# A decoder layer with product-key experts: the second half of the tokens computes every expert in dense matmul steps instead of gathering its own

## What is computed

```python
def peer_ffn(h, w_q, keys1, keys2, u_tab, v_tab):
    q = (hf @ w_q).astype(jnp.float32).reshape(tokens, PEER_HEADS, 2, PEER_HALF)
    s1 = jnp.einsum('thd,hnd->thn', q[:, :, 0], keys1.astype(jnp.float32))
    s2 = jnp.einsum('thd,hnd->thn', q[:, :, 1], keys2.astype(jnp.float32))
    v1, i1 = lax.top_k(s1, PEER_TOPK)
    v2, i2 = lax.top_k(s2, PEER_TOPK)
    ...
    top_score, pos = lax.top_k(cand_score, PEER_TOPK)
    expert_id = jnp.take_along_axis(cand_id, pos, axis=-1)
    gate = jax.nn.softmax(top_score, axis=-1)
    ...
        u_sel = u_tab[idb].astype(jnp.float32)
        act = jax.nn.gelu(jnp.einsum('tkd,td->tk', u_sel, xb.astype(jnp.float32)), approximate=False)
        return jnp.einsum('tk,tkd->td', gb * act, v_tab[idb].astype(jnp.float32))
```

## Time and profile before

| | us |
|---|---|
| median of 2 runs | 1733.03 |
| the runs | 1725.96, 1740.11 |
| span of the profiled execution (first to last instruction) | 1657.0 |
| PE busy | 1355.5 (82%) |
| DVE busy | 1063.8 (64%) |
| POOL busy | 775.5 (47%) |
| ACT busy | 348.9 (21%) |
| moved by DMA | 599.35 MB, mean 362 GB/s |

### The profile page before, as it was taken

The page is one execution under the profiler, slowest core; times in us unless marked ns, Lnnn a source line. Parts: engine busy times, 40 slices in busy tenths (PEclk is TensorE's granted clock), DMA queues, the critical chain, the costliest instruction groups (busy, mean ns, idle before and its releaser), DMA issues.

```text
span 1657.0 us, 16021 instructions
## 1 busy us (share of the span) xinstructions
PE 1355.5 (82%) x5078; PEld 669.4 (40%) x5078; DVE 1063.8 (64%) x2871; ACT 348.9 (21%) x776; POOL 775.5 (47%) x848
## 2 busy tenths in 40 slices
PE   8999899888788978877769876678877778788777
PEld 7866574432455644642213320122332333333323
DVE  4625249957777889976555766444565666666656
ACT  2321422211342322011002120021122222222221
POOL 3000005766676657775467777355433333334332
PEclk9999999999998989997779997689999998998999
DMA  4223807999999999999999999999999999999995
GB/s 154 77 102 115 299 25 269 380 411 412 409 409 409 411 396 409 408 409 411 398 411 409 409 410 411 418 412 417 420 422 422 421 421 422 422 421 422 421 422 224
DMA packets 130212, 599.35 MB, mean 362 GB/s; under 512 B 15824, under 2 KB 15824, under 8 KB 97360
## 3 DMA queue, kind: packets, MB, share of 16 engines
q0 software_dynamic: 115776, 536.92, 80.3%
q1 hardware_dynamic: 14208, 61.15, 9.6%
q10 hardware_dynamic: 144, 0.26, 0.0%
HBM read 596.18 MB, written 2.10 MB: 361 GB/s over the span
## 4 chain that ended last, share of the span: by engine, by line
DMA 44%; PE 27%; DVE 12%; POOL 8%; issue 6%; ACT 2%; DVEq 1%; ACTq 0%; SPq 0%; POOLq 0%
DMA arena<-in_peer_uv,arena 21%; DMA arena<-in_peer_v,arena 14%; DMA arena<-in_peer_u,arena 9%; PE psum L1152 7%; DVE arena L1906 5%; POOL arena L752 4%; POOL arena L740 4%; PE psum L1130 4%; PE psum L1083 3%; PE psum L816 3%; PE psum L827 3%; PE psum L1064 2%; DVE arena L1537 1%; ACT arena L1428 1%; PE psum L838 1%
## 5 line engine op out<-in xcount | busy, mean ns | idle before, releaser
L1906 DVE CUSTOM_DVE_ANT_0 arena<-arena,psum 128x1024 f32<-128x1024 f32 x512 | 622.9, 1218 | 417.7 <-DMA arena<-in_peer_uv,arena 245.8
L1152 PE MATMUL psum<-arena 128*128 128x512 f32 x880 | 426.5, 642 | 98.3 <-ACT arena L1428 98.3
L740 POOL DMA_INDIRECT arena<-in_peer_u,arena x288 | 272.4, 946 | 363.4 <-PE psum L893 226.0
L1130 PE MATMUL psum<-arena 128*32 128x512 f32 x1152 | 278.5, 726 | 128.6 <-DMA arena<-in_peer_v,arena 128.5
L772 POOL DMA_INDIRECT arena<-in_peer_uv,arena x220 | 207.1, 941 | 335.2 <-PE psum L1152 299.1
L752 POOL DMA_INDIRECT arena<-in_peer_v,arena x288 | 271.5, 943 | 147.1 <-issue 76.8
L1152 PEld LDWEIGHTS psum<-arena 128*128 128x128 f32 x880 | 176.1, 205 | 352.6 <-issue 217.7
L1130 PEld LDWEIGHTS psum<-arena 128*32 128x32 f32 x1152 | 47.3, 120 | 313.9 <-DMA arena<-in_peer_v,arena 224.1
L816 PE MATMUL psum<-arena 128*128 128x512 f32 x256 | 118.5, 609 | 2.5 <-DVE st L1579 2.4
L1083 PE MATMUL psum<-arena 128*128 128x512 f32 x224 | 98.7, 593 | 1.4 <-ACT arena L1355 1.4
L827 PE MATMUL psum<-arena 128*128 128x256 f32 x384 | 93.0, 402 | 8.3 <-ACT arena L1211 7.0
(11 more groups left out here) (271 smaller groups left out, 1395.0 us busy)
## 6 DMA issues: line engine op xcount, KB each, us to landing
arena<-in_w_in SPq DMA_DIRECT2D x28, 1024.0 KB, 7.8
arena<-in_w_out SPq DMA_DIRECT2D x16, 512.0 KB, 7.9
arena<-in_peer_w_q SPq DMA_DIRECT2D x16, 512.0 KB, 14.0
arena<-in_peer_w_q SPq DMA_DIRECT2D x8, 1024.0 KB, 13.2
arena<-in_peer_u,arena POOLq DMA_INDIRECT x292, 15.5
arena<-in_peer_v,arena POOLq DMA_INDIRECT x292, 15.9
arena<-in_peer_uv,arena POOLq DMA_INDIRECT x220, 27.3
arena<-in_x SPq DMA_DIRECT2D x4, 512.0 KB, 5.1
```

What stands on the lines that cost most here:

```text
L740: pool.indirect_dma_start(row, None, u_d, bass.IndirectOffsetOnAxis(ap=eid[i % 2][:, c:c + 1], axis=0)).then_inc(landed, 16)
L1130: mm = pe.matmul(bank[6 + half][group * UK:(group + 1) * UK], zrows[k % 2][:, z0:z0 + ZW], row[:, half * 512:(half + 1) * 512], start=Fals ...
L1152: mm = pe.matmul(bank[y_bank[i][half]], diag_w[q % 2][:, j], row[:, D + half * 512:D + (half + 1) * 512], start=False, stop=c == SEL - 1 o ...
L1906: dve.tensor_tensor_reduce(row, row, h2p[i], 1.0, 0.0, ALU.mult, ALU.add, dots[:, c:c + 1]).then_inc(s["u_free"], 1)
```

## The change

Rows 0 to 255 (tiles 0 and 1, `GATHERED`) are gathered and computed as before, v rows in the 32-column form. `peer_uv`, `gather_pair`, `quad_rows`, `spread_quad`, `scale_quad` and the late adds are gone.

Tiles 2 and 3 are computed together, over all 16,384 experts, in 64 **dense steps** of 2 x 128 experts after the row loop. `peer_ut` is the u table transposed and split by step, made on the host ahead of the launch. A step has:

- `u`: 16 matmuls, weight 128 (width) x 128 (experts) of `peer_ut`, 256 moving columns (the tokens of both tiles, `h2T_both`), into one bank
- Gelu on ACT from PSUM to `wd`, then on DVE `wd` times the gate matrix `G` (128 experts x 256 tokens x 2), zero where an expert was not chosen
- `v`: 8 matmuls, weight 128 (experts) x 128 (tokens) of `wd`, 512 moving columns of the v table, added up over all steps in four banks, which start from xs (`yd`)

`G` is made from the choices in two parts of 64 second keys, 32 batches each (`g`): for each of 8 tokens DVE makes a one-hot matrix of the first key times the gate (`pick`, 128x128), and for four tokens at once the one-hot of the second key (`place_`, 128 x 4 x 64); PE multiplies them over the selections, ACT copies the bank to `G`. `pick` and `place_` have two buffers of four tokens. Part 0 is placed in the row loop, at rows 213 to 220 for tile 2 and 258 to 265 for tile 3; part 1 in the dense steps, two batches after each `u` from the sixth on.

SP loads each step's 1 MB of u and 1 MB of v (two u buffers; four early and two late v buffers).

In `places()` every row n beyond 40 becomes 40 + (n - 40) * 2 // 3: the last step stands at row 190 instead of 266. The choices of tile 1, begun at rows 108 to 206 before, begin at 98 to 154, two links a row. The choices of tiles 2 and 3 have 11 links each, two in a row, from row 167 (`dense_choices`), followed by the gates (`gate`) and a transposition to selections on partitions (`kt`).

```diff
-CHOOSE_AT, CHOOSE_EVERY = SEL - 20, 14
-LINKS = 13
+CHOOSE_EVERY = 14
+SECOND_AT, SECOND_EVERY = 98, 8
+LINKS, DENSE_LINKS = 13, 11
+GATHERED = GT * SEL
...
+    sooner = {}
+    for n in sorted(at):
+        sooner.setdefault(n if n <= BEGIN else BEGIN + (n - BEGIN) * 2 // 3, []).extend(at[n])
+    return sooner
...
+def dense_choices(at):
...
+    for t in range(GT, NT):
+        for h in range(PH):
+            for link in range(DENSE_LINKS):
+                if n <= place["s", t, h // 2]:
+                    n, room = place["s", t, h // 2] + 1, 0
+                if room == (2 if n < GATHERED else DENSE_LINKS):
+                    n, room = n + 1, 0
+                LINK_AT.setdefault(n, []).append((t, h, link))
+                room += 1
...
+def dense_steps():
+
+    later = [("g", 1, b) for b in range(BATCHES)]
+    out = [("yd", t, half) for t in DENSE_T for half in range(2)] + [("u", 0, 0), ("u", 0, 1)]
+    for n in range(STEPS):
+        out.append(("v", 0, n))
+        if n + 2 < STEPS:
+            out.append(("u", 0, n + 2))
+        if n >= 4:
+            out += later[2 * (n - 4):2 * (n - 3)]
+    return out
...
+            def load_tables(n):
+
+                slot = n % len(U_SLOT_KB)
+                if n == 0:
+                    sp.wait_ge(*filled("s", NT - 1, PH // 2 - 1))
+                elif n == 1:
+                    sp.wait_ge(*linked(NT - 1, PH - 1, 1))
+                else:
+                    sp.wait_ge(*filled("u", 0, n - 2))
+                sp.dma_start(u_slot[slot], peer_ut[n]).then_inc(ut_in[slot], 16)
+                slot, turn_ = v_slot(n)
+                if n < 4:
+                    sp.wait_ge(s["u_free"], GATHERED)
+                elif n < V_EARLY:
+                    sp.wait_ge(s["v_done"], n - 3)
+                elif n < V_EARLY + 2:
+                    sp.wait_ge(s["v_free"], GATHERED)
+                else:
+                    sp.wait_ge(s["v_done"], n - 1)
+                sp.dma_start(v_slots[slot], v_step_d[n].rearrange("i (j d) -> i j d", j=STEP_KEYS)).then_inc(vt_in[slot], 16)
...
-            for n in range(NT * SEL):
-                if n >= PAIRS:
-                    gather_pair(n)
-                else:
+            for n in range(GATHERED + LAG):
+                if n < GATHERED:
                     gather_u(*divmod(n, SEL))
...
+                elif kind == "g":
+                    ps = claim("g", t, i)
+                    if t:
+                        pe.wait_ge(s["y_out"], 2 * GT)
+                    for q in range(BATCH // SUB):
+                        m = (t * BATCHES + i) * (BATCH // SUB) + q
+                        pe.wait_ge(s["ab_rdy"], m + 1)
+                        for j in range(SUB):
+                            k = q * SUB + j
+                            mm = pe.matmul(ps[:, k * PASS_KEYS:(k + 1) * PASS_KEYS], pick[m % 2][:, j], place_[m % 2][:, j], start=True, stop=True)
+                        if q < BATCH // SUB - 1:
+                            mm.then_inc(s["ab_used"], 1)
...
+                elif kind == "u":
+                    ps = claim("u", 0, i)
+                    slot = i % len(U_SLOT_KB)
+                    pe.wait_ge(ut_in[slot], 16 * (i // len(U_SLOT_KB) + 1))
+                    for k in range(STEP_KEYS):
+                        for c in range(DC):
+                            mm = pe.matmul(ps[:, 2 * P * k:2 * P * (k + 1)].rearrange("p (t c) -> p t c", t=2), u_slot[slot][:, k, c],
+                                           h2T_both[:, :, c * P:(c + 1) * P], start=c == 0, stop=c == DC - 1)
+                    mm.then_inc(filled("u", 0, i)[0], 1)
+                elif kind == "v":
+                    slot, turn_ = v_slot(i)
+                    pe.wait_ge(s["w_rdy"], i + 1)
+                    pe.wait_ge(vt_in[slot], 16 * turn_)
+                    for k in range(STEP_KEYS):
+                        end = i == STEPS - 1 and k == STEP_KEYS - 1
+                        for a, tt in enumerate(DENSE_T):
+                            for half in range(2):
+                                mm = pe.matmul(bank_for("yd", tt, half), wd[i % 2][:, k, a * P:(a + 1) * P],
+                                               v_slots[slot][:, k, half * 512:(half + 1) * 512], start=False, stop=end, skip_group_check=True)
...
+                        for j in range(SUB):
+                            dve.tensor_scalar(pick[m % 2][:, j], keyno, key[:, 0, n + j:n + j + 1], key[:, 2, n + j:n + j + 1], ALU.is_equal, ALU.mult)
+                        dve.tensor_tensor(place_[m % 2], keyno[:, t * PASS_KEYS:(t + 1) * PASS_KEYS].unsqueeze(1).to_broadcast([P, SUB, PASS_KEYS]),
+                                          key[:, 1, n:n + SUB].unsqueeze(2).to_broadcast([P, SUB, PASS_KEYS]), ALU.is_equal).then_inc(s["ab_rdy"], 1)
...
+                    dve.wait_ge(*read("u", 0, i))
+                    dve.tensor_tensor(w, w, G[part][:, :, first:first + STEP_KEYS].rearrange("p t k -> p k t"), ALU.mult).then_inc(s["w_rdy"], 1)
```

More of the change, by code:

```diff
@@ L116, in consumed, with v_slot, batch_tokens @@
                 out["v", k * UK + jj] = count
[L117 to L121, removed]
     return out
 CONSUMED = consumed()
[L128 to L146, removed]
+PASS_KEYS = NKEYS // 2
+STEP_KEYS = 2
+STEPS = NKEYS // STEP_KEYS
+DENSE_T = (3, 2)
+SUB = 4
+BATCH = 512 // PASS_KEYS
+BATCHES = 2 * P // BATCH
+U_SLOT_KB = (130, 122)
+V_EARLY_KB, V_EARLY = (48, 56, 64, 72), 8
+V_LATE_KB = (203, 80)
+IOTA_AT = 200
+def v_slot(s):
+    if s < V_EARLY:
+        return s % 4, s // 4 + 1
+    return 4 + s % 2, (s - V_EARLY) // 2 + 1
+def batch_tokens(part, b):
+    t = (DENSE_T[::-1] if part == 0 else DENSE_T)[b // (BATCHES // 2)]
+    return t, b % (BATCHES // 2) * BATCH
 def spread(main, extra):
@@ L370, in layer_kernel @@
             USE[step + (0,)] = USE["proj", step[1], step[2] - 2, 0]
-        turn += len(got) == 1 and step[0] not in ("kk", "x", "mk", "nw", "qk", "y", "mv", "vn", "os", "st", "z", "o")
-    BEFORE_USES = {b: max(n for step, (bb, n) in USE.items() if bb == b) for b in range(8)}
+        turn += len(got) == 1 and step[0] not in ("kk", "x", "mk", "nw", "qk", "y", "mv", "vn", "os", "st", "z", "o", "g", "u", "yd")
     UNITS_DONE = [step for step in ORDER if step[0] == "proj" and unit(step[1], step[2])[0] in CHANNELS]
@@ new lines, in dense @@
+            def dense(kind, t, i):
+                if kind == "yd":
+                    ps = claim("yd", t, i)
+                    pe.wait_ge(s["u_free"], GATHERED)
+                    pe.wait_ge(*read("wo", t, i))
+                    pe.matmul(ps, ident[:], xs[:, t, i * 512:(i + 1) * 512], start=True, stop=False, skip_group_check=True)
+                elif kind == "u":
[14 more added lines that the diff above has]
+                        for a, tt in enumerate(DENSE_T):
+                            for half in range(2):
+                                mm = pe.matmul(bank_for("yd", tt, half), wd[i % 2][:, k, a * P:(a + 1) * P],
+                                               v_slots[slot][:, k, half * 512:(half + 1) * 512], start=False, stop=end, skip_group_check=True)
+                                if end:
+                                    mm.then_inc(s["yd_done"], 1)
+                    if i < STEPS - 1:
+                        mm.then_inc(s["v_done"], 1)
+                else:
+                    step_(kind, t, i)
@@ L1169, in _ @@
                 k, j = divmod(n - LAG, UK)
-                if 0 <= k < PAIRS // UK and j % NQ == NQ - 1:
+                if 0 <= k < GATHERED // UK and j % NQ == NQ - 1:
                     rows(k, j - NQ + 1)
-                q = (n - QUAD_ROWS - PAIRS) // QUAD
-                if (n - QUAD_ROWS) % QUAD == 0 and 0 <= q < QUADS:
-                    quad_rows(q)
+            for step in DENSE:
+                dense(*step)
         @block.scalar
```

367 lines of the change are left out of this document (182 added, 185 removed).

## The result

| | before | after |
|---|---|---|
| median of 2 runs, us | 1733.03 | 2324.20 |
| the runs | 1725.96, 1740.11 | 2323.67, 2324.74 |
| span of the profiled execution | 1657.0 | 2321.9 |
| moved by DMA, MB | 599.35 | 465.52 |

The change makes the kernel slower: 1.3455 times the time before, 95% interval 1.3232 to 1.3678. The forecast had the direction and the larger part of the loss, and was 141 us too low, outside its range. When both kernels were measured again, on other chips, before took 1655 and after 2225 us: the same ratio, with both some 5% shorter.

A forecast was written before the change was run, and what follows sets the result against it. DMA gathers of table rows were taken as the bound. Row 256 at 956 + 25 + 36 + 61 = 1078 us, + 1024 dense stage + 5 tail = 2107 span, + 76 around it = 2183 us; range 2090 to 2262.

The forecast's parts named there:

- a plain dense step: Dense stage: 32 records at 0.216 and 16 at 0.429 make 13.8 us of PE, 883 us for 64 steps.
- rival 4: Dense matmuls: records start twice as fast, stage 442 us shorter, 1741 us in all, not slower; chance 0.03.
- the tables: Dense stage: each step's 2 MB of u and v tables load hidden beneath 13.8 us of PE, at 152 GB/s.
- Rival 3: Dense stage: tables come late through SP's in-order waits, +115 us, 2298 us in all; chance 0.07.
- the shortened distance: Rows 40 to 190: the second group's moved steps make PE and DMA level and cost +25 us, bounds 0 and +80.
- Rival 2: Row loop: engines wait in order, +80 instead of +25, DVE jam +60 instead of +36, 2262 us; chance 0.18 with another rival.
- 76 us lie around: Outside the span: before's median 1733.0 less its span 1657.0, added to the forecast span of 2107 us.
- the jam in rows 213 to 220: Row loop: two batches of G a row take DVE 58 us where DMA needs 21; +36 us (20 to 60).
- rows 256 to 292: End of row loop: 36 v rows and first tables take 61 us at 410 GB/s, tile 3's batches lying beneath.
- part 1 in the dense steps: Sixteen dense steps: building G adds 7.6 us each, 122 us, plus 16 us for the fallen clock.
- The upper price, 146: Building part 1 of G in the dense steps, with 0.27 us picks and hand-overs to match: 146 us instead of 122.
- rival 1: Dense steps: G hides, part 1 costs only PE's own 57 us and no clock, 2102 us in all; chance 0.13.

The follow-up runs named there:

- e9: After with no G at all, neither in the row loop nor in the dense steps; output not the reference's: 1941.28 us, ratio 1.1707.
- e4: After without the 32 batches of part 1 of G, all 64 products taking part 0; output not the reference's: 2037.58 us.
- e3: Before with only the second group's steps at two thirds of their distance and tile 1's choices where after has them: 1687.81 us, ratio 1.0209.
- e10: After with the second group's steps at five sixths of their distance, tile 1's choices from row 108 every 11 rows: 2235.53 us, ratio 1.3477.
- e2: After measured once more, no edit: 2224.98 us, ratio 1.3444.
- e1: Before measured once more, no edit: 1656.02 us, ratio 1.0002.
- e6: After with tile 3's batches of part 0 at every second row instead of two a row: 2205.1 us, ratio 1.3307.
- e5: After with part 1 of G ahead of u, one batch a step, in 31 dense steps instead of 16: 2094.36 us, ratio 1.2644.
- e11: After measured a third time, no edit: 2223.77 us, ratio 1.3438.
- e12: Before measured a third time, no edit: 1658.95 us, ratio 1.0011.

## Why the prediction was right and wrong

**Right: a plain dense step, 13.8 us, 883 in all.** This was the term said to decide. PE in after, one plain step:

```profile
1296.39 7.07 PE L1200 MATMUL psum<-arena 128*128 128x256 f32 x32
1303.30 7.03 PE L1211 MATMUL psum<-arena 128*128 128x512 f32 x16
1310.16 7.07 PE L1200 MATMUL psum<-arena 128*128 128x256 f32 x32
```

From 1296.39 to 1310.16 are 13.77 us: 32 records at 0.216 and 16 at 0.429, as the chain of before had them. The counts of records are those foreseen, 2048 and 1024. e9 makes the stage 882 us with nothing else in it. So the gathers' 655 us were given for 883 on PE, and rival 4 is dead. By the Trainium skill's gap formula ("TensorE: Matmul & The Clock Gate", Back-to-back issue gap), taken for each record, the step would have been half as long; the trace disagrees with that for float32 records, by a factor of two.

**Right: the tables.** They land in 6.8 and 4.7 us, at about 150 GB/s in the dense stage, and no dense matmul waits for one (e4: PE 395 of 395 us). Rival 3 is dead.

**Right, a little low: the shortened distance, +25.** e3 measured +33 in all and 27 at row 256, and e10 takes nothing off. Rival 2's +80 is dead. Row 190 stood at 822 us in e2, where the prediction's 462 us and its 25 lead to 817.

**Wrong: the last step of the sum, "76 us lie around" the span.** Around the span lie 2 us (e1: 1660.2 and 1658.3; after: 2323.67 and 2321.9). The step subtracted the span of one execution from the times of others. The 76 us were, as far as e1 tells, longer executions beside a shorter profiled one. The table of before could have warned: its own two executions differ by 14 us, so one more could differ too, and a difference between executions is no fixed cost. The Trainium skill ("Runtime: NRT & Kernel Launch", The ~15µs preamble/postamble breakdown) speaks of some 6.2 us by which a profile's total exceeds the reported time. That is another pair of quantities: here the span from the first to the last instruction is below the reported time, by about 2 us, and neither is near 76. What the first measurement had in addition was about 5% of either kernel (ratios 1.3455 and 1.3444); for after it lay wholly in the row loop (102 us), and where it lay in before no trace shows, so that the ratios agree may be chance. Without this step the sum is 2107 against a span of 2220: the rest was 113 us too low, and the 76 hid that in part: that 2225 falls inside the range is luck. The whole account of the 141 us is 113, plus the 102, less 76, plus the 2 around the span. As a ratio, 2107 by 1657 is 1.27, and 1.344 was measured.

Most of the 113 us are the terms for `G`: building it in the row loop and in the dense steps was priced too low in three places.

**Mis-sized: the jam in rows 213 to 220, and the reason given for it.** It was priced at 58 us as DVE's time. It took 76 (882 to 958 us), and row 256 came at 1041 instead of 1017. PE in e2, three rows of it:

```profile
885.59 7.29 PE L1183 MATMUL psum<-arena 128*128 128x64 f32 x32 [2.25 <-DVE arena L1875]
894.75 7.29 PE L1183 MATMUL psum<-arena 128*128 128x64 f32 x32 [1.87 <-DVE arena L1875]
903.78 7.29 PE L1183 MATMUL psum<-arena 128*128 128x64 f32 x32 [1.74 <-DVE arena L1875]
```

A row takes 9.1 us, of which 7.3 are PE's. The prediction had 7.2 for the row with DVE setting the pace and PE's two batches as 3.6, taken from a row at full clock. At the granted clock of this stretch, 0.54 (0.50 in 885 to 911 us, the lower of its two levels), each record of 64 columns takes 0.23 us instead of 0.11. So DVE and PE hand the four-token buffers to and fro, and both are nearly full (65 and 63 of 76 us). DVE's own 65 are 7 over the price, since a pick is 0.26 us and not 0.21; the other 11 are waits. PE had been busy 37 of 60 us in the stretch before. What the jam costs at row 256 is less: the rows behind it catch up (35 in 83 us, 2.4 each). In e9, without the batches, row 256 comes at 1000 us, so they cost 41 us there, where the sum had 36. The other 19 of the 24 us are in e9 too, whose row 256 is 44 us behind before's 956 where 25 were forecast: e3 has 27 of these 44 with the moved steps alone. The rest, some 17, e9 has with the choices of tiles 2 and 3 on top, for which the sum put nothing beside the jam; that they are the cause is not shown, and five executions of the same row loop differ by 11 us at row 256 (1040 to 1051).

**Mis-sized: rows 256 to 292, 102 us instead of 61** (105 to the first u, less 3.7 for the copies of xs, which the prediction counts with the dense stage). The prediction laid tile 3's batches "beneath" the last v gathers because DVE's sum of 43 us was shorter. It left out PE's queue. The waits of POOL in 1041 to 1146 us (total, times, longest), and PE in two pieces of that stretch:

```profile
POOL arena L838 <- PE psum L1244: 63.5, 6, 26.7
```

```profile
1050.00 10.94 PE L1183 MATMUL psum<-arena 128*128 128x64 f32 x48
1060.87 3.64 PE L1244 MATMUL psum<-arena 128*32 128x512 f32 x16
1064.44 2.49 PE L1183 MATMUL psum<-arena 128*128 128x64 f32 x16
...
1117.44 1.04 PE L1244 MATMUL psum<-arena 128*32 128x512 f32 x2 [1.73 <-DMA arena<-in_peer_v,arena]
```

POOL's v gathers (L838) want a buffer that PE's v rows (L1244) give back, and those stand behind `g` in PE's order. POOL stands still for 63.5 of 105 us. When the batches are done, from 1117 on, PE waits for single rows: the gathers that were not issued are now made up for. e9 has neither and takes 58 us from row 256 to the first u (54 without the copies), and the gathers run at 393 GB/s: for a kernel without `g` the 61 were 7 too many, and `g` costs 47 here. Spreading these batches alone (e6) gave back 20, less than the 30 to 45 expected of it, so how the 47 divide between the place of the batches and the time they take at the low clock (0.67) stays open.

**Mis-sized: part 1 in the dense steps, 122 + 16 us.** e4 measures 187. The step of e2 shown under e5, the first of the sixteen, is 25.9 us (their mean is 24.7), 12.1 over a plain one: 3.2 of waiting (2.8 was forecast), 6.6 from the first record of `g` to v (4.8), and v itself 9.0 instead of 6.9 (1). DVE in the same step:

```profile
1229.65 1.03 DVE L1979 TENSOR_TENSOR arena<-arena 128x512 f32<-128x512 f32 x1 [12.73 <-ACT arena L1482]
1230.59 1.11 DVE L1874 TENSOR_SCALAR arena<-tri_gt,arena 128x128 f32<-128x128 f32 x4
1231.62 0.42 DVE L1875 TENSOR_TENSOR arena<-tri_gt,arena 128x256 f32<-128x256 f32 x1
1231.95 1.11 DVE L1874 TENSOR_SCALAR arena<-tri_gt,arena 128x128 f32<-128x128 f32 x4
...
1233.73 1.12 DVE L1874 TENSOR_SCALAR arena<-tri_gt,arena 128x128 f32<-128x128 f32 x4 [0.33 <-PE psum L1183]
```

The product takes 1.03 instead of 0.69, four tokens 1.36 (1230.59 to 1231.95) instead of 1.2: a pick is 0.26 from start to start, close to the upper bound of the range and not the 0.21 that was chosen. But from the third four on DVE waits for PE, not PE for DVE: again the 64-column records at 0.21. The clock was put down at 1 us a gap, for v alone; it was worth about 2 in v and as much in `g`. Busy time of PE, PEld, DVE, ACT and POOL in two parts of that v, with the granted clock behind them:

```profile
1238.00:1243.00 5.00, 5.00 (x10) 2.56 (x10) 0.00 (x0) 0.58 (x1) 0.00 (x0) 0.50 0.01 3
1243.00:1248.00 5.00, 5.00 (x13) 2.28 (x12) 0.00 (x0) 0.00 (x0) 0.00 (x0) 1.00 0.00 0
```

The clock is 0.50 from 1235 on, in `g` and in the first part of v, and back at 1.00 after that. The upper price, 146, would not have reached either: it took the first four at 1.2 us and only the others at 1.8. e5 supports the prediction's reading of the order (product first, then picks, with PE behind them both): with the picks ahead of time the wait, the clock and 131 us go, and the 56 that are left are rival 1's price for part 1 (57).

Put together: 24 us to row 256, 41 behind it and 50 in the dense stage (1074 from the copies on, 1024 forecast), less 2 in the tail (3 instead of 5), are the 113. About 95 of them are `G`'s: 5, 41 and 50. In all `G` costs 284 us (e9) where the prediction had 138 in the dense steps and some 36 in the row loop. Rival 1 asked whether `G` hides; part 1 costs just what rival 1 says when it stands elsewhere and one batch at a time (e5), but not in this order.

Open is what stretched the first measurement by 5%. The trace of after gives "issue" or an unknown queue for the pauses, and neither e2, e11, e1 nor e12 had them.

## What to carry to other kernels

Where bytes are traded for matmuls, count the records of the new loop and multiply by the start-to-start time of the same record shape in the old trace; that one product decided this case and came out to 1%. Price small helper work by its place in the in-order queues (who stands behind it, how many buffers lie between, whether its input is ready when the engine gets there), and price its matmuls at the lower granted clock if the engine will wait there: here it cost 284 us, where its own length on PE at full clock is 64 batches of 1.8, 115 us, and placing half of it ahead of u, one batch a step, gave back 131. And never take the difference of one execution's span and another execution's time as a cost of the launch.

## What the runs showed of the hardware

- A float32 record of 64 columns with a full 128x128 weight takes 0.12 us at granted clock 1.00 (e5: 16 in 1.89) and 0.23 at 0.54 (e2: 32 in 7.29). Its weight loads average 303 ns in after, against 202 beneath the wider records.
- With pauses of 3.2 us ahead of such records the granted clock was 0.82 over 395 us in which PE was busy 340; with no pause (e4, e5) it was 1.00. Within the first such step of e2 it was 0.50 for 8 us (1235 to 1243), then 1.00.
- DVE's product of 128x512 with `G`, which it reads at a stride, took 1.04 us (64 times, mean 1043 ns), where a product of the same size, with one input in PSUM, took 0.69. That the stride is the cause was not tried.
- `tensor_scalar` over 128x128 with two scalars from memory: 347 ns each, 0.26 us from start to start.
- One execution of the same program can be 5% longer than another with engines standing still for up to 11 us on DVE and 30 on ACT, for which the trace names no instruction or known queue as the releaser (after against e2).
